# A recurrent layer streamed as one loop of six weight tiles, and one function set on ScalarE through the norms

## What is computed

```
def rglru_block(h, w_in, conv_w, conv_b, w_a, b_a, w_i, b_i, lam, w_out):
    xb, yb = jnp.split(h @ w_in, 2, axis=-1)
    gate = jax.nn.gelu(yb, approximate=True)
    xb = causal_dwconv(xb, conv_w, conv_b)              # 4 taps along the tokens
    xh = xb.reshape(B, T, LRU_BLOCKS, LRU_BLOCK_DIM)    # 8 blocks of 256 channels
    r = sigmoid(einsum('bthi,hij->bthj', xh, w_a) + b_a)
    i = sigmoid(einsum('bthi,hij->bthj', xh, w_i) + b_i)
    log_a = -LRU_C * r * softplus(-lam)
    a = jnp.exp(log_a)
    u = jnp.sqrt(-jnp.expm1(2.0 * log_a)) * (i * xb)
    hs = scan over tokens of  s = a * s + u
    return (hs * gate) @ w_out
```

## Time and profile before

| | us |
|---|---|
| three runs, median (lowest to highest) | 3485.86 (3480.83 to 3489.13) |
| the profiled execution | 3488.29 |
| its span in the profile | 3486.5 |
| mean granted clock of PE | 0.963 of full speed |

### The profile page before, as it was taken

How to read it: one execution, slowest core, us unless ns; L and a number is a source line. 1 busy time by engine, 2 the same in 40 slices (tenths; PEclk the granted TensorE clock), 3 DMA queues, 4 the chain that set the end, 5 groups by cost and what they waited for, 6 DMA issues and landing times.

```text
span 3486.5 us, 52830 instructions
## 1 busy us (share of the span) xinstructions
PE 3232.7 (93%) x18216; PEld 2795.4 (80%) x18216; DVE 2397.9 (69%) x3704; ACT 1767.3 (51%) x2265; POOL 13.1 (0%) x20
## 2 busy tenths in 40 slices
PE   7889999999999996699999999998779989999997
PEld 6778888888888885578888888887667768888876
DVE  6556786676687657777767767876455777666665
ACT  5664554454455446645544544544444554444443
POOL 1000000000000000000000000000000000000000
PEclk9889999999999998899999999999889999999998
DMA  5223555555555542345555555554223434444543
GB/s 186 90 82 139 182 192 184 190 181 187 188 191 181 182 173 96 103 168 190 183 182 191 182 184 190 192 181 156 97 97 116 150 132 169 169 170 167 174 151 121
DMA packets 83046, 561.20 MB, mean 161 GB/s; under 512 B 9728, under 2 KB 12800, under 8 KB 15872
## 3 DMA queue, kind: packets, MB, share of 16 engines
q1 hardware_dynamic: 82944, 559.87, 45.5%
HBM read 557.73 MB, written 2.10 MB: 161 GB/s over the span
## 4 chain that ended last, share of the span: by engine, by line
PE 72%; DVE 14%; issue 6%; ACT 5%; DMA 2%; DVEq 1%; ACTq 0%; SPq 0%
PE unit L277 44%; PE unit L278 22%; DVE w_tail L950 5%; DVE prod L956 1%; ACT w_head L648 1%; DMA raw<-in_wo 1%; DMA raw<-in_lru_x 1%; PE o L340 1%; ACT lo L655 1%; DVE pr L1124 1%; PE s L320 1%; ACT L744 0%; PE tr L331 0%; ACT L664 0%; DVE mx L998 0%
## 5 line engine op out<-in xcount | busy, mean ns | idle before, releaser
L277 PE MATMUL unit<-h,w_head 128*128 128x512 f32 x5552 | 2004.6, 405 | 37.5 <-DVE kv L1244 33.2
L278 PE MATMUL unit<-h,w_tail 128*128 128x256 f32 x5552 | 1567.8, 282 | 0.0
L648 ACT ACTIVATE w_head<-raw 128x2048 fp32r<-128x2048 f32 (+1 forms) x540 | 1013.3, 1876 | 598.0 <-DMA raw<-in_up 203.9
L277 PEld LDWEIGHTS unit<-h,w_head 128*128 128x128 f32 x5552 | 1060.2, 191 | 300.2 <-DVE kv L1244 36.5
L950 DVE TENSOR_TENSOR w_tail<-raw,w_head 128x2048 fp32r<-128x2048 f32 (+1 forms) x540 | 1209.3, 2240 | 11.6
L278 PEld LDWEIGHTS unit<-h,w_tail 128*128 128x128 f32 x5552 | 1064.7, 192 | 2.6
L277 PE MATMUL unit<-act,w_head 128*128 128x512 f32 x2528 | 896.5, 399 | 21.4 <-DVE act L967 14.1
L956 DVE TENSOR_TENSOR prod<-unit,lo 128x256 f32<-128x256 f32 x508 | 215.4, 424 | 730.0 <-ACT lo L655 725.0
L278 PE MATMUL unit<-act,w_tail 128*128 128x256 f32 x2528 | 710.9, 281 | 0.0
L277 PEld LDWEIGHTS unit<-act,w_head 128*128 128x128 f32 x2528 | 477.6, 189 | 140.6 <-DVE act L967 16.6
L278 PEld LDWEIGHTS unit<-act,w_tail 128*128 128x128 f32 x2528 | 480.4, 190 | 0.2
(11 more groups left out here) (195 smaller groups left out, 1847.9 us busy)
## 6 DMA issues: line engine op xcount, KB each, us to landing
raw<-in_up SPq DMA_DIRECT2D x192, 1024.0 KB, 4.8
raw<-in_down SPq DMA_DIRECT2D x96, 1024.0 KB, 4.8
raw<-in_odd SPq DMA_DIRECT2D x64, 1024.0 KB, 4.8
raw<-in_even_b SPq DMA_DIRECT2D x32, 1024.0 KB, 4.8
raw<-in_attn SPq DMA_DIRECT2D x24, 1024.0 KB, 4.9
raw<-in_wo SPq DMA_DIRECT2D x16, 1024.0 KB, 4.8
raw<-in_lru_y SPq DMA_DIRECT2D x16, 1024.0 KB, 4.8
raw<-in_lru_x SPq DMA_DIRECT2D x16, 1024.0 KB, 4.8
```

The source lines that it names most:

```text
L277: pe.matmul(bank[:, :], w_head[:, slot, at], src[:, k, :], start=k == 0, stop=False)
L278: last = pe.matmul(bank[:, 0:SEQ], w_tail[:, slot, at], src[:, k, 0:SEQ], start=False, stop=k == KT - 1)
L648: a.activation(w_head[:, slot, 0:width], raw[:, r, 0:width], ACT.Copy).then_inc(head_done, 1)
```

## The change

Two parts. First, `preload_act_table_set(LN_EXP)` puts a set that holds logarithm and exponential together in place at the start, and again ahead of each phase whose last unit is followed by a layer's norm (`lru_out`, the last down projections, `even_out`, `odd_out`). Second, `lru_y` and `lru_x` become one phase `lru` of 8 blocks of six units in the order x, y, x, y, gate, gate, written out without a loop. PE takes the x and y units as three matmuls a step, so all three parts are summed in one half bank; `lo_half` and `product` fall away, and DVE scales straight from the bank (`lru_taken`). The gates use the two score banks. ACT and DVE work on both gate tiles of a block together, one block later. The first two units of `lru_out` run side by side and take each k as its tile comes.

```diff
+LN_EXP = "natural_log_exp_and_others"
...
-          + [("lru_y", 16), ("lru_x", 32), ("lru_out", 16)]
+          + [("lru", 48), ("lru_out", 16)]
...
+            def stream_lru():
+                for i in range(LRU_BLOCKS):
+                    u, m = BASE["lru"] + LRU_UNITS * i, 2 * i
+                    for j, (src, tile) in enumerate((("lru_x", m), ("lru_y", m), ("lru_x", m + 1), ("lru_y", m + 1))):
+                        load(t[src][tile], u + j, j)
...
-                    load(t["lru_g"][KT - 2 + j], b + 30 + j, j, GATE_W)
+                        load(t["lru_g"][m + j], u + 4 + j, j, GATE_W)
...
+            def lru_unit(u, freed, first=False):
+                slot, bank = u % RING, unit_bank[u % 2]
                 pe.wait_ge(tail_done, u + 1)
-                pe.wait_ge(bank_free, u - 1)
+                pe.wait_ge(bank_free, freed)
+                for k in range(KT):
...
+                    pe.matmul(bank[:, 0:SEQ], w_head[:, slot, at], h[:, k, 0:SEQ], start=k == 0, stop=False)
+                    pe.matmul(bank[:, 0:SEQ], w_head[:, slot, at], h[:, k, SEQ:2 * SEQ], start=False, stop=False)
+                    last = pe.matmul(bank[:, 0:SEQ], w_tail[:, slot, at], h[:, k, 0:SEQ],
+                                     start=False, stop=k == KT - 1)
+                last.then_inc(unit_done, 1)
+            def lru_gate(u, s, tile0):
+                slot = u % RING
+                pe.wait_ge(tail_done, u + 1)
+                pe.wait_ge(bank_free, u - 5)
...
-                    out = bank[:, kind * SEQ:(kind + 1) * SEQ]
+                    out = ps_s[s][:, kind * SEQ:(kind + 1) * SEQ]
...
+            for i in range(LRU_BLOCKS):
+                u = BASE["lru"] + LRU_UNITS * i
+                for j in range(4):
+                    lru_unit(u + j, u + j - (3 if i and j < 2 else 1), i == 0 and j == 0)
+                    if i == 0 and j == 0:
+                        token_norm(2)
+                pe.wait_ge(act_done, ACTS["lru"] + 2 * i + 2)
+                for s in range(2):
+                    lru_gate(u + 4 + s, s, 2 * i)
...
             for j in range(2):
-                unit(b + j, j, h)
-            with pe.Fori(1, LRU_BLOCKS) as i:
+                pe.wait_ge(tail_done, b + j + 1)
+                pe.wait_ge(bank_free, b + j - 3)
+                for k in range(KT - 2):
+                    pe.wait_ge(lru_d, k + 1)
+                    out_step(j, k)
...
+            for k in range(KT - 2, KT):
+                pe.wait_ge(lru_d, k + 1)
                 for j in range(2):
-                    unit(i * 4 + (b - 2 + j), 2 + j, h)
-                pe.wait_ge(act_done, i * 2 + ACTS["lru_x"])
...
+                    last = out_step(j, k)
+                    if k == KT - 1:
+                        last.then_inc(unit_done, 1)
...
+            a.preload_act_table_set(LN_EXP)
...
+                if final and name != "wo":
+                    a.preload_act_table_set(LN_EXP)
...
+                u = BASE["lru"] + LRU_UNITS * i + j
+                split(u, u, GATE_W if i < LRU_BLOCKS and j >= 4 else D_MODEL)
...
+            def lru_conv(i, s):
+                m = 2 * i + s
+                a.wait_ge(bank_free, BASE["lru"] + LRU_UNITS * i + 2 * s + 1)
+                a.activation(kv[:, 2 + s, :], kv[:, s, :], ACT.Identity,
                              scale=lru[:, m, L_W3:L_W3 + 1], bias=lru[:, m, L_B:L_B + 1]).then_inc(conv_init, 1)
...
+            def lru_gelu(i, s):
+                a.wait_ge(bank_free, BASE["lru"] + LRU_UNITS * i + 2 * s + 2)
+                a.activation(store[:, 2 * i + s, :], kv[:, 4 + s, :], ACT.Gelu_apprx_tanh).then_inc(gelu_done, 1)
...
+            def lru_tanhs(i):
+                for s in range(2):
+                    m = 2 * i + s
+                    a.wait_ge(unit_done, BASE["lru"] + LRU_UNITS * i + 4 + s + 1)
+                    if i:
+                        a.wait_ge(lru_d, m - 1)
+                    a.activation(pr[:, s, 0:SEQ], ps_s[s][:, 0:SEQ], ACT.Tanh, scale=0.5, bias=hb[:, 0, m:m + 1])
+                    a.activation(pr[:, s, SEQ:2 * SEQ], ps_s[s][:, SEQ:2 * SEQ], ACT.Tanh, scale=0.5,
+                                 bias=hb[:, 1, m:m + 1]).then_inc(lru_tanh, 1)
...
+            def lru_decay(i):
+                a.wait_ge(lru_tanh, 2 * i + 2)
+                for s in range(2):
+                    m = 2 * i + s
+                    a.activation(prt[:, s * SEQ:(s + 1) * SEQ], pr[:, s, 0:SEQ], ACT.Exp, scale=spl[:, 0, m:m + 1],
+                                 bias=spl[:, 0, m:m + 1]).then_inc(lru_exp, 1)
+                for s in range(2):
+                    m = 2 * i + s
+                    a.activation(lo[:, s, :], pr[:, s, 0:SEQ], ACT.Tanh, scale=spl[:, 1, m:m + 1],
+                                 bias=spl[:, 1, m:m + 1])
+                a.wait_ge(lru_exp, 2 * i + 2)
+                for s in range(2):
+                    a.activation(kv[:, 6 + s, :], prt[:, s * SEQ:(s + 1) * SEQ], ACT.Square).then_inc(lru_sq, 1)
+            def lru_roots(i):
+                for s in range(2):
+                    a.wait_ge(lru_sum, 2 * i + s + 1)
+                    a.activation(kv[:, 6 + s, :], kv[:, 6 + s, :], ACT.Sqrt).then_inc(lru_root, 1)
...
+            lru_split(0, 3)
+            for i in range(LRU_BLOCKS):
+                if i:
+                    lru_split(i, 3)
+                    lru_decay(i - 1)
+                lru_conv(i, 0)
+                lru_split(i, 4)
+                if i:
+                    lru_roots(i - 1)
+                lru_gelu(i, 0)
+                lru_split(i, 5)
+                lru_conv(i, 1)
+                lru_split(i + 1, 0)
+                lru_gelu(i, 1)
+                lru_split(i + 1, 1)
+                lru_tanhs(i)
+                lru_split(i + 1, 2)
+            lru_decay(LRU_BLOCKS - 1)
+            lru_roots(LRU_BLOCKS - 1)
+            a.wait_ge(lru_d, KT)
...
+            def lru_taken(i, j, dst):
+                u = BASE["lru"] + LRU_UNITS * i + j
+                v.wait_ge(unit_done, u + 1)
+                v.scalar_tensor_tensor(dst, unit_bank[u % 2][:, 0:SEQ], 1.0, rstd[:, :], ALU.mult, ALU.mult)\
+                    .then_inc(bank_free, 1)
...
+            def lru_conv(i, s):
+                m = 2 * i + s
+                xb = kv[:, 2 + s, :]
+                v.wait_ge(conv_init, CONVS["lru"] + m + 1)
+                for back_by, w in enumerate((L_W2, L_W1, L_W0), 1):
+                    link(v.scalar_tensor_tensor(xb[:, back_by:SEQ], kv[:, s, 0:SEQ - back_by], lru[:, m, w:w + 1],
+                                                xb[:, back_by:SEQ], ALU.mult, ALU.add))
+                split_act(m, xb).then_inc(act_done, 1)
...
+            def lru_inputs(i):
+                for s in range(2):
+                    v.wait_ge(lru_tanh, 2 * i + s + 1)
+                    v.scalar_tensor_tensor(pr[:, s, SEQ:2 * SEQ], pr[:, s, SEQ:2 * SEQ], 1.0, kv[:, 2 + s, :],
+                                           ALU.add, ALU.mult).then_inc(bank_free, 1)
...
+            def lru_sums(i):
+                for s in range(2):
+                    v.wait_ge(lru_sq, 2 * i + s + 1)
+                    v.scalar_tensor_tensor(kv[:, 6 + s, :], kv[:, 6 + s, :], 1.0, lo[:, s, :], ALU.add, ALU.mult)\
+                        .then_inc(lru_sum, 1)
...
+            def lru_scan(i, s):
+                m, decay, into = 2 * i + s, prt[:, s * SEQ:(s + 1) * SEQ], pr[:, s, SEQ:2 * SEQ]
...
+                v.wait_ge(bank_free, BASE["lru"] + LRU_UNITS * i + LRU_UNITS)
+                link(v.scalar_tensor_tensor(into, kv[:, 6 + s, :], 0.5, into, ALU.mult, ALU.mult))
+                link(v.tensor_tensor_scan(kv[:, 6 + s, :], decay, into, 0.0, ALU.mult, ALU.add))
+                v.wait_ge(gelu_done, GELUS["lru"] + m + 1)
+                link(v.tensor_tensor(into, kv[:, 6 + s, :], store[:, m, :], ALU.mult))
+                v.wait_ge(unit_done, BASE["lru"] + LRU_UNITS * i + LRU_UNITS)
+                split_act(m, into).then_inc(lru_d, 1)
+            lru_tail(0, 3)
+            for i in range(LRU_BLOCKS):
+                if i:
+                    lru_inputs(i - 1)
+                    lru_tail(i, 2)
+                lru_taken(i, 0, kv[:, 0, :])
+                if i:
+                    lru_tail(i, 3)
+                    lru_sums(i - 1)
+                lru_conv(i, 0)
+                lru_taken(i, 1, kv[:, 4, :])
+                lru_tail(i, 4)
+                if i:
+                    lru_scan(i - 1, 0)
+                lru_tail(i, 5)
+                lru_taken(i, 2, kv[:, 1, :])
+                lru_conv(i, 1)
+                lru_tail(i + 1, 0)
+                lru_taken(i, 3, kv[:, 5, :])
+                if i:
+                    lru_scan(i - 1, 1)
...
+                lru_tail(i + 1, 1)
+            lru_inputs(LRU_BLOCKS - 1)
+            lru_tail(LRU_BLOCKS, 2)
+            lru_sums(LRU_BLOCKS - 1)
+            for s in range(2):
+                lru_scan(LRU_BLOCKS - 1, s)
```

(1 more changed line is left out.)

144 lines of the change are left out of this document (36 added, 108 removed).

## The result

The changed kernel takes 3363.53 us (median of 4 runs, 3358.61 to 3367.44) against 3485.61 for the kernel before on the same chip: a ratio of 0.9653, 95% interval 0.9636 to 0.9671. The forecast was 3380 with a range of 3345 to 3418. The direction and the recurrent layer came as forecast; some 16 us more were gained than that, and the query tiles are where most of them lie.

The account below looks back on a forecast made before the run. PE bounds the kernel (busy 93%), so gains come only where it waits or runs at low clock. 5.5 + 36 + 57 + 6 + 1.3 = 106 off 3488.3 gives 3382, the median 2.4 lower: 3380 us, range 3345 to 3418.

Parts of the forecast that it names:

- The ring: Recurrent layer: dependent transfers, ACT and DVE passes, two places of `raw`, set a block at 29.1 us; layer -57.
- The rival in which PE is the bound: Recurrent layer: the ring does not bind, PE does, at 25.7 us a block; 3357 us, chance 8 in 100.
- The longer ring: Recurrent layer: two transfers in flight slow each other, a block takes 33 us; 3410 us, chance 14 in 100.
- PE staying at 1.2 GHz in the blocks: Recurrent layer: PE drops to 1.2 GHz at each block's two waits and stays there; 3556 us, chance 3 in 100.
- The query tiles, -36 forecast: First attention: table loads removed from the chain and some clock regained, 2.25 us a tile, 36 us in 16.
- Start and key units: First attention's start: 3.2 us less at the first key unit and 2.3 in the three behind it, together 5.5.
- some of it comes back: Query tiles: part of the 1.7 us a tile lost to low clock returns once PE's wait is a few tenths.
- that rows show: Query tiles, lower end: 1.86 us a tile (30 us) if the clock does not rise; the forecast stayed near it.
- 2.9 (46 us) if it does throughout: Query tiles, upper end: 2.9 us a tile, 46 us in all, if PE's clock rises throughout.
- The fourth layer, -6 forecast: Entry and later norm waits need no load: 2.6 at the first head norm, about 0.9 and 2.6 later.
- Loads at 0 in the feed-forward parts: Loads ahead of residual phases and at the first GELU or tanh afterwards cost 0, as PE does not wait there.
- The drain of a table load: Skill's rule: about 1380 ns of drain, 2.66 us a switch, adding 11 us in the ring; 3391, chance 2 in 100.

Follow-up runs that it names:

- e4_two_products: The changed kernel with two of the three matmuls a step in the recurrent layer's 32 x and y units; 3382.74 us in one execution.
- e6_ring_order: e5_decay_first with DVE's order in a block changed too (sums and several tails earlier, first convolution later), no instruction added or removed; 3348.8 us, ratio 0.9588.
- e2_stream_only: The changed kernel without the three places that load the set with logarithm and exponential, the one-stream recurrent layer kept; 3435.07 us, ratio 0.9832.
- e9_load_in_idle_time: The changed kernel with one table load per query tile put behind the softmax's last exponential, where ACT is idle; 3369.22 us in one execution.
- e5_decay_first: The changed kernel with ACT's decay step of the block before put ahead of the split of the block's fourth unit; 3357.6 us, ratio 0.9599.
- the closing edit: Third output unit's split and tail moved behind the last block's roots and scans, run with e6_ring_order and a fourth-layer load edit; together 3339.24 us, ratio 0.9554.

## Why the prediction was right, and where its sizes were off

*The recurrent layer, -57 forecast, -59.7 measured.* The ring was the right mechanism and nearly the right size: 29.1 a block against 28.7, and PE's waits stand where the text put them, 1.3 to 1.97 before the fourth unit (about 2 forecast) and 0.76 before the gates (about 1), with the fourth unit's head pass waiting for its transfer. e4_two_products rules out PE as the bound, and e6_ring_order shows that the ring's length is queueing: with each transfer and pass unchanged, an order with less ahead of the passes takes 2.4 us out of a block. The rival in which PE is the bound failed as a forecast of this kernel and came true for the reordered one, at 25.9 and more a block: the prediction's 25.7 takes a unit of 48 starts at 5.7 where 48 x 0.12 is 5.76. The longer ring, and PE staying at 1.2 GHz in the blocks, did not come: the blocks ran at 1.00.

*The query tiles, -36 forecast, some -47 measured.* This is the term that was mis-sized. Start and key units gave 7.3 of the first stretch's 54.4 (forecast 5.5), the rest is tiles. The chain was right in kind: PE's waits fell by 21.6, but that is 1.35 a tile and not 1.86, because 0.65 of wait is left in each. What failed is the step "some of it comes back", with 0.39 a tile for the clock and a preference for the end "that rows show". The clock came back in full, 0.87 to 1.00, and PE's busy time fell by 26.2 (173.73 to 147.58), some 1.6 a tile. A tile gained 2.90. That is the upper end of the bounds ("2.9 (46 us) if it does throughout"), but the bound was made of 1.86 of wait and 1.0 of clock, so it is luck that the two together meet it so closely. Three runs say why the clock came back. With waits of 0.65 or 1.76 a tile it is 1.00, with waits of 3.04 it is 0.87 and the slow part falls on the matmuls that ACT waits for. The clock isn't given back in proportion to the wait: once the wait is short, all of it is.

*The fourth layer, -6 forecast, -15.1 measured.* One profile misleads here. In two profiles with the old loads (before and e2_stream_only) the layer took 570.0 and 568.4, of which PE waited 91.7 and 92.1. In the nine with the new ones it took 558.0 in the mean and PE waited 85.7. So the waits fell by 6.2, which is the term of the sum; PE's busy time fell by 5.0, most of it clock (granted 0.916 before, 0.926 in the mean of the nine), which the sum left out; and the changed kernel's own profile was the lowest of the nine, 3 us under their mean in both length and waits.

*Last norm, -1.3 forecast, -1.5 measured*; the load is gone from ACT:

```profile
3338.01 0.47 ACT L702 ACTIVATE rstd<-norm,lamb 128x256 f32<-128x256 f32 x1 [1.31 <-PE norm L289]
3338.52 0.42 ACT L703 ACTIVATE rstd<-rstd 128x256 f32<-128x256 f32 x1
```

*Loads at 0 in the feed-forward parts.* Nothing speaks against it: +0.7 and -0.7, and e9_load_in_idle_time shows by itself that a load where ACT is idle costs nothing.

*The drain of a table load* stays unseen: the activation behind a load starts 1.29 or 1.30 after the load did, in the trace of before for 120 of 127 loads, and behind the others it waits for something else. The trace decides against the rule's 2.66.

## What to carry to other kernels

Price a stall on TensorE's chain twice, once for its length and once for the clock that follows it, and work the second out at both ends: where PE's wait went from 0.65 to 1.76 us a table load cost 1.1, where it went on to 3.04 the same load cost 2.8. Look at the single waits too, since a mean can hide two forms. Before shortening an engine's work, see what stands ahead of the instruction that frees a buffer: here the same instructions in another order were worth 2.4 us of a 28.7 us block, while a third less matmul work was worth nothing. Where an execution's own spread is several us, cut the span at fixed instructions and compare stretches; the ratios of e5_decay_first and e6_ring_order differ by 0.001, with intervals that overlap, and their recurrent stretches by 10 us. Cut finely enough: the closing edit's 1.3 us looked like 4.2 as long as the whole recurrent stretch was compared.
